# Latent attention with the plain rows of two heads and the rotary rows of four in shared tiles, and dense tiles at one address modulo 256

## What is computed

```python
h = x @ w_in[l]
c_q, c_kv, k_r, gate_a, q_d, k_d, v_d, gate_b, gates = _split_cols(h)
q_a = (_rms_norm(c_q, g_q[l]) @ w_q_up[l]).reshape(b, s, 8, 64 + 32)
q_a = jnp.concatenate([q_a[..., :64], _rotary(q_a[..., 64:], 32)], axis=-1)
kv = (_rms_norm(c_kv, g_kv[l]) @ w_kv_up[l]).reshape(b, s, 8, 64 + 64)
k_rope = _rotary(k_r, 32)                       # one for all heads
k_a = jnp.concatenate([kv[..., :64], jnp.broadcast_to(k_rope[:, :, None, :], (b, s, 8, 32))], axis=-1)
o_a = _dense_attention(q_a, k_a, kv[..., 64:], 1 / math.sqrt(96))   # softmax over all 512 keys
y_a = (o_a * jax.nn.silu(gate_a)) @ w_branch_a[l]
```

## Time and profile before

| | us |
|---|---|
| median of 3 runs (3389.13 to 3394.4) | 3393.46 |
| the profiled execution | 3391.75 |
| its span, first to last instruction | 3388.7 |
| TensorE busy | 3245.6 (96%) |
| VectorE busy | 2087.4 (62%) |
| GpSimd busy | 1347.1 (40%) |
| ScalarE busy | 1182.2 (35%) |
| mean granted TensorE clock, share of full | 0.977 |

### The profile page before, as it was taken

The page is one execution under the profiler, slowest core; times in us unless marked ns, Lnnn a source line. Parts: engine busy times, 40 slices in busy tenths (PEclk is TensorE's granted clock), DMA queues, the critical chain, the costliest instruction groups (busy, mean ns, idle before and its releaser), DMA issues.

```text
span 3388.7 us, 43762 instructions
## 1 busy us (share of the span) xinstructions
PE 3245.6 (96%) x16074; PEld 2541.7 (75%) x16074; DVE 2087.4 (62%) x2758; ACT 1182.2 (35%) x1808; POOL 1347.1 (40%) x565
## 2 busy tenths in 40 slices
PE   8999999999996999999998999999998999989998
PEld 6666787666785888778677888878887876878887
DVE  3877785777785444898378443464459964774422
ACT  3354423354423222433444222432233335332233
POOL 3302343302342445634143444634454531534454
PEclk9999999999997999999999999999998999999999
DMA  4524482524472332577232332333235771423332
GB/s 135 166 76 125 128 252 75 162 84 126 127 223 73 100 98 80 97 117 98 60 106 81 103 96 81 105 87 98 85 90 86 119 111 32 140 75 99 91 85 72
DMA packets 577891, 359.50 MB, mean 106 GB/s; under 512 B 48898, under 2 KB 528588, under 8 KB 577484
## 3 DMA queue, kind: packets, MB, share of 16 engines
q1 hardware_dynamic: 573908, 351.02, 40.3%
q10 hardware_dynamic: 3832, 6.42, 0.5%
HBM read 344.53 MB, written 10.49 MB: 105 GB/s over the span
## 4 chain that ended last, share of the span: by engine, by line
PE 51%; DVE 12%; SPq 2%; DMA 2%; issue 1%; ACT 1%; POOL 1%; ACTq 0%; POOLq 0%; DVEq 0%
PE bank L158 16%; PE bank L160 16%; PE bank L159 16%; SPq L1725 2%; DVE w_s L2349 2%; DMA w_raw<-in_mix_w_in_dram 1%; DVE xT L2464 1%; DVE z_s L2349 1%; DVE tt_s L2349 1%; DVE ct_s L2349 1%; PE bank L2030 1%; PE bank L2009 1%; POOL w_lo L152 1%; DVE y_s L2452 1%; DVE th_s L2471 0%
## 5 line engine op out<-in xcount | busy, mean ns | idle before, releaser
L152 POOL TENSOR_TENSOR w_lo<-w_raw,w_hi 128x1024 fp32r<-128x1024 f32 (+2 forms) x552 | 1339.1, 2432 | 2004.0 <-ACT w_hi L144 1996.0
L158 PE MATMUL bank<-xh,w_lo 128*128 128x512 f32 x2432 | 974.1, 401 | 46.4 <-DVE xl L2429 26.7
L160 PE MATMUL bank<-xh,w_hi 128*128 128x512 f32 x2432 | 962.3, 396 | 0.0
L159 PE MATMUL bank<-xl,w_hi 128*128 128x512 f32 x2432 | 960.8, 395 | 0.0
L144 ACT ACTIVATE w_hi<-w_raw 128x1024 fp32r<-128x1024 f32 (+2 forms) x552 | 565.9, 1028 | 788.9 <-PE bank L160 683.1
L158 PEld LDWEIGHTS bank<-xh,w_lo 128*128 128x128 f32 x2432 | 461.8, 190 | 167.4 <-issue 46.9
L159 PEld LDWEIGHTS bank<-xl,w_hi 128*128 128x128 f32 x2432 | 462.3, 190 | 104.5 <-issue 4.3
L160 PEld LDWEIGHTS bank<-xh,w_hi 128*128 128x128 f32 x2432 | 461.8, 190 | 99.3
L158 PE MATMUL bank<-HH_s,w_lo 128*128 128x512 f32 x704 | 276.1, 392 | 0.0
L160 PE MATMUL bank<-HH_s,w_hi 128*128 128x512 f32 x704 | 275.7, 392 | 0.0
L159 PE MATMUL bank<-HL_s,w_hi 128*128 128x512 f32 x704 | 275.0, 391 | 0.0
(11 more groups left out here) (509 smaller groups left out, 4392.1 us busy)
## 6 DMA issues: line engine op xcount, KB each, us to landing
w_raw<-in_ffn_w_in_dram SPq DMA_DIRECT2D x176, 512.0 KB, 3.9
m_raw_l<-in_mod_w_dram SPq DMA_DIRECT2D x128, 512.0 KB, 5.0
w_raw<-in_w_in_dram SPq DMA_DIRECT2D x80, 512.0 KB, 4.0
w_raw<-in_mix_w_in_dram SPq DMA_DIRECT2D x64, 512.0 KB, 9.9
w_raw<-in_ffn_w_out_dram SPq DMA_DIRECT2D x64, 384.0 KB, 3.4
w_raw<-in_ffn_w_out_dram SPq DMA_DIRECT2D x64, 320.0 KB, 3.2
m_half_l<-in_mod_w_dram SPq DMA_DIRECT2D x32, 256.0 KB, 2.7
w_raw<-in_w_out_dram SPq DMA_DIRECT2D x16, 512.0 KB, 4.8
```

What stands on the lines that cost most here:

```text
L152: nc.gpsimd.tensor_tensor(ring.lo[s][:, 0:width], ring.raw[s][:, 0:width], ring.hi[s][:, 0:width].bitcast(F32), ALU.subtract).then_inc(rin ...
L158: nc.tensor.matmul(out, wl, xh, start=start, stop=False)
L159: nc.tensor.matmul(out, wh, xl, start=False, stop=False)
L160: return nc.tensor.matmul(out, wh, xh, start=False, stop=stop)
```

## The change

It has three parts.

1. Tiles. `QT` becomes `QN` (4 tiles: plain rows of two heads, 128 rows) and `QR` (2 tiles: rotary rows of four heads), `KTr` becomes `KN` (4 tiles) and `KR` (one tile with the 32 rotary key rows four times). Block 3 now loads 32 columns, and `split_hi` and `split_lo` write them four times. The two query blocks are split in two instructions on each engine, which pack the columns. The query blocks take 3 groups of 6 matmuls of 128 columns each, the key block 4 of 3, and the swaps go from 16 to 10. The ScalarE spread and its semaphore go.
2. Scores. `scores_a(g)` now makes both heads of pair g: two matmuls of 64 rows at rows 0 and 64 of QN and KN, then two of 32 rows added onto them. It is issued after the transposes of an odd j, for g = j // 2 + 2. Score banks go from 3 to 4. The modulation's turn and column copy move (`half_turns`, `half_columns`).
3. Addresses. `eps` and `mod_cols` move behind xl, five small tiles become one of 32 bytes, and `mem.align()` puts the large tiles of both blocks at the ring's place modulo 256.

The diff, cut to its core:

```diff
-def split_hi(nc, act, ring, n, quad, s, width):
+def split_hi(nc, act, ring, n, quad, s, parts):
...
-    nc.scalar.activation(ring.hi[s][:, 0:width], ring.raw[s][:, 0:width], ACT.Copy).then_inc(ring.hi_done, 1)
+    for of, to in parts if isinstance(parts, list) else whole(parts):
+        ins = nc.scalar.activation(to(ring.hi[s]), of(ring.raw[s]), ACT.Copy)
+    ins.then_inc(ring.hi_done, 1)
...
+        if n == 3:
+            return [(lambda x: x[:, 0:KT * ROPE].rearrange("p (k a c) -> p k a c", k=KT, a=1).broadcast_to([P, KT, P // ROPE, ROPE]),
+                     lambda x: x[:, 0:BLK].rearrange("p (k a c) -> p k a c", k=KT, a=P // ROPE))]
+        if B_UP <= n < B_UP + 2:
...
+            return [(raw(slice(0, NOPE)), packed(0, NOPE)), (raw(slice(NOPE, QK)), packed(4 * NOPE, ROPE))]
...
-    half_turns = {17: 4, 30: 5}
-    half_columns = {20: 4}
+    half_turns = {16: 4, 30: 5}
+    half_columns = {17: 4, 31: 5}
...
     for j in range(NA):
-        hold(("s", j), j % 3)
-        hold(("t", j), 3 + j % 2)
+        if j in half_turns:
+            hold(("mod", half_turns[j]), 7)
+        hold(("s", j), j % 4)
+        hold(("t", j), 4 + 3 * (j % 2))
...
         for b in range(2):
             wh, wl = weights(B_UP + b, b)
             pe.wait_ge(s_cn, 2)
-            for h in range(4 * b, 4 * b + 4):
-                out = free(pe, ("qh", h))
+            for i, label in enumerate((("qn", 2 * b), ("qn", 2 * b + 1), ("qr", b))):
+                out = free(pe, label)
                 for k in range(2):
-                    c = slice(k * 384 + (h % 4) * QK, k * 384 + (h % 4) * QK + QK)
-                    last = mm3(nc, out[0:QK, :], wh[:, c], wl[:, c], cnh[:, k, :], cnl[:, k, :], k == 0, k == 1)
+                    c = slice(k * 384 + i * P, k * 384 + (i + 1) * P)
+                    last = mm3(nc, out, wh[:, c], wl[:, c], cnh[:, k, :], cnl[:, k, :], k == 0, k == 1)
...
+            out = [free(pe, ("s", 2 * g + side)) for side in range(2)]
+            c = slice(q * P, (q + 1) * P)
+            for side in range(2):
+                r = slice(side * NOPE, (side + 1) * NOPE)
+                nc.tensor.matmul(out[side], QN[r, p, c], KN[r, p, :], start=True, stop=False)
+            for side in range(2):
+                first = (2 * p + side) % 4 * ROPE
+                r = slice(first, first + ROPE)
+                nc.tensor.matmul(out[side], QR[r, p // 2, c], KR[r, :], start=False, stop=True).then_inc(s_sc, 1)
...
-            if j + 3 < NA:
-                scores_a(j + 3)
             pe.wait_ge(s_p, j + 1)
             turn_probs(("t", j), PX[j % 4])
+            if j % 2 and j // 2 + 2 < NA // 2:
+                scores_a(j // 2 + 2)
             if j >= 2:
                 attend_a(j // 2 - 1, (0, 1) if j % 2 == 0 else (2, 3))
...
         for j in range(NA):
             if j + 2 < NA:
                 negmax_a(j + 2)
+            if j in half_columns:
+                mod_columns(half_columns[j])
             wait_read(dve, ("s", j))
...
+    def align(self):
+        self.at += (self.phase - self.at) % self.LINE
```

More of the change, by code:

```diff
@@ L136, in fetch, with whole @@
     sp.dma_start(dst, src).then_inc(ring.load[s], 16)
-def split_hi(nc, act, ring, n, quad, s, width):
+def whole(width):
+    return [(lambda x: x[:, 0:width], lambda x: x[:, 0:width])]
+def split_hi(nc, act, ring, n, quad, s, parts):
     act.wait_ge(ring.load[s], 16 * quad + 16)
@@ L151, in split_lo @@
         pool.wait_ge(ring.used, n - (RING - 1))
-    nc.gpsimd.tensor_tensor(ring.lo[s][:, 0:width], ring.raw[s][:, 0:width],
-                            ring.hi[s][:, 0:width].bitcast(F32), ALU.subtract).then_inc(ring.lo_done, 1)
+    for of, to in parts if isinstance(parts, list) else whole(parts):
+        ins = nc.gpsimd.tensor_tensor(to(ring.lo[s]), of(ring.raw[s]), to(ring.hi[s]).bitcast(F32), ALU.subtract)
+    ins.then_inc(ring.lo_done, 1)
 def mm3(nc, out, wh, wl, xh, xl, start, stop):
@@ L495, in source @@
             if n < B_UP:
-                first = ([0, P, 2 * P, C_KR - NOPE] + [C_QD + m * P for m in range(4)] + [C_KD + m * P for m in range(4)])[n]
-                return w[:, :, first:first + P]
+                first = ([0, P, 2 * P, None] + [C_QD + m * P for m in range(4)] + [C_KD + m * P for m in range(4)])[n]
+                return w[:, :, first:first + P] if n != 3 else w[:, :, C_KR:C_KR + ROPE]
             if n < B_VD:
@@ L634, in mod_turn, with swap @@
             last.then_inc(s_mturn, 1)
-        def swap(i, src, rot, rows=slice(0, P)):
-            out = free(pe, ("r", i))
-            nc.tensor.matmul(out[rows, :], rot[rows, rows], src, start=True, stop=True).then_inc(s_rotated, 1)
+        def swap(i, src, rot):
+            nc.tensor.matmul(free(pe, ("r", i)), rot, src, start=True, stop=True).then_inc(s_rotated, 1)
         for s in range(4):
@@ L719, in turn_probs, with scores_a @@
             last.then_inc(s_tr, 1)
-        def scores_a(j):
-            p, q, side, h = place(j)
+        def scores_a(g):
+            p, q = divmod(g, TT)
             if q == 0:
[L725 to L730, removed]
+                pe.wait_ge(s_rot, 9 + p // 2)
+                wait_read(pe, ("qn", p))
+                wait_read(pe, ("kn", p))
+                if p == 0:
+                    pe.wait_ge(s_kr, 1)
+            out = [free(pe, ("s", 2 * g + side)) for side in range(2)]
[7 more added lines that the diff above has]
+                nc.tensor.matmul(out[side], QR[r, p // 2, c], KR[r, :], start=False, stop=True).then_inc(s_sc, 1)
         def attend_a(i, keys):
@@ L747, in attend_a @@
                         ins.then_inc(s_att, 1)
-        for j in range(3):
-            scores_a(j)
+        scores_a(0)
+        scores_a(1)
         for j in range(NA):
@@ L1014, in hi_next @@
                 act.wait_ge(ring.used, B_END + n - (RING - 1))
-                split_hi(nc, act, after.ring, n, 0, n, BLK)
+                split_hi(nc, act, after.ring, n, 0, n, width(n))
         for m in range(KT):
@@ L1435, in second_block @@
     pick = mem("pick", [P, HF], F32R)
+    mem.align()
     big = mem.at
@@ L2805 @@
 class Memory:
+    LINE = 256
     def __init__(self, nc, base, end):
-        self.nc, self.at, self.end, self.place, self.tag = nc, base, end, {}, ""
+        self.nc, self.at, self.end, self.place, self.tag, self.phase = nc, base, end, {}, "", 0
+    def align(self):
+        self.at += (self.phase - self.at) % self.LINE
     def __call__(self, name, shape, dtype, over=None, skip=0):
```

111 lines of the change are left out of this document (52 added, 59 removed).

## The result

The changed kernel takes 3401.55 us (median of 20 runs, 3397.41 to 3405.29), the kernel before 3394.86 (20 runs beside them, 3387.91 to 3400.93). The ratio is 1.0017, interval 1.001 to 1.0023: 3.4 to 7.8 us slower. The forecast was 0.6 us slower, so no change. The time lies in the range, but the change is real and the forecast had none. The profiled execution took 3403.22 us with a span of 3401.4, 12.7 more than before; 2.45 of these lie ahead of the first dense product (15.82 before, 18.27 after), among them a second wait of 1.43 us for a load of the input, which the kernel before does not have.

What follows compares the result with a forecast made beforehand. TensorE's own queue plus its few waits was taken to bound the kernel. To 3391.75 us came -24.4 (latent stage), -20 (addresses) and +45 (latent attention), +0.6 in all: about 3392 us, range 3369 to 3413.

Steps and rivals of the forecast that it cites:

- Part 1: Latent stage: fewer, wider products and fewer swaps take 16.43 us instead of 28.62, -12.2 us per layer, -24.4 for both.
- Rival (e): Latent stage: its saving is eaten by a wait for a split or a copy, up to 24 us, 3416; chance 0.04.
- Part 2: Latent attention, TensorE's own work: each score pair 1.06 us, a whole pair 4.48 against 4.16, +5 us per layer.
- Rival (d): Latent attention: the two 32-row products run one behind the other, 27 us, 3419 us, slower; chance 0.06.
- Part 3: Latent attention: TensorE waits for VectorE's normalise, 0.87 us in 14 groups (+12.2 per layer) and 0.67 eight times (+5.4).
- Rival (a): Latent attention: TensorE's new wait is smaller; half gone 3371 us, wholly hidden 3357; chance 0.28, of it 0.26 faster.
- rival (c): Latent attention: idle brings five stretches per layer of granted clock below full, 16 us, 3408 us, slower; chance 0.09.
- its own sign of being wrong: Latent attention: the prediction called itself wrong if the granted clock there falls under 0.95.
- part 4: Dense product and values stage: big tiles level modulo 256 bytes shorten the pitch, -20 us, between -15 and -26.
- Rival (b): Dense product: place in a partition is not the cause, the address term is 0, 3412 us, slower; chance 0.11.

Runs made afterwards that it cites:

- the normalise first: The changed kernel with VectorE's normalise of j (and a half chunk) moved ahead of the maximum for j + 2: 3362.88 us, ratio 0.9897 to the kernel before.
- the scores earlier: The changed kernel with a group's scores issued ahead of the transposes of the odd j instead of behind them: 3369.68 us, ratio 0.9924 to the kernel before.
- the waits filled: The changed kernel with matmuls of no use put into TensorE's waits in the latent attention: 3396.38 us, ratio 0.9997 to the kernel before.

## Why the prediction was wrong, step by step

**Part 1 held.** -12.2 per layer forecast, 28.62 to 16.55 measured, -12.1. Rival (e), a wait for a split or a copy, did not come.

**Part 2 held.** Both score pairs 1.06; the pair without waits 4.47 against 4.48. Rival (d) fell: the 32-row products run side by side, even four of them. This is what the Trainium skill, "TensorEngine Tiling (Array Packing)", section Key Properties, says of tiles, and rows now show it for 32 rows. The change of height costs about 0.20 where it was measured alone.

**Part 3 held as a mechanism and in size.** Waits at the places named, behind the releaser named, 0.85 and 0.68 from start to start for 0.87 and 0.67. Undone from VectorE's side they go (the normalise first), from TensorE's side they shrink by exactly the cover that is added (the scores earlier). Rival (a) fell.

**The step that failed: the clock was left out of the sum.** The prediction put parts 2 and 3 at 22.6 per layer and gave the clock to rival (c), at 0.09, with the argument that "the idle comes between full-speed 512-column scores". That argument holds for the steady loop and not for its start, where the profile of the changed kernel has 1.37 us idle, transposes alone, 0.54 idle. There the lower level begins and lasts 10 us. It costs 3.5 us in each layer (95.7 against 92.15 with the waits filled), 7.1 in both; the kernel before lost 1.6 in layer 0. So the attention windows are 95.7 where the prediction wanted 91 to 93, and their granted clock prints as 0.95, right at its own sign of being wrong. The rival priced its stretches by the one before, 1.6 each, and counted as decisive only from five in both layers together (8 us); two, each three times as long, cost 7.1 and were enough to turn no change into a clear one. What exactly brings the clock down is shown only so far: it fell in both layers of all four kernels that have 1.37 us idle, transposes alone and 0.54 idle at the start (the changed one, the one without the addresses and the two with x moved), and in none where the first wait was short (0.19), where scores stood behind it, or where the waits were filled.

**Mis-sized, if at all here: part 4.** The pitch came out as forecast, 228.75 to 226.67. The term was 20; the runs show 14 (9 to 19) and 15 (9 to 20) on the kernel before, and 17 (12 to 22) on the changed one. On the kernel before, the sum took for granted that the clock stays as it was. On the changed one no such loss shows: its mean clock of 0.9726 is 0.0025 under the kernel before, and its attention stages alone make that up (0.05 of 191 us less 0.02 of 71 us is 8 us of 3400, an estimate), so 20 is not excluded there. Rival (b) is out. It rested on the rule of the Trainium skill, "SBUF — State Buffer", section SBUF: two separate sides, that TensorE's port waits on nobody. The pitch follows the place of the two operands all the same, 226.67 to 233.7 ns for the same products, and the measurement decides.

With the measured sizes: -24.1 - 17.3 + 51.3 = +9.9. The two profiled executions fit that: 12.7 apart in span, 2.45 of it ahead of the first product, so 10.2. The medians show 3.4 to 7.8. Of the difference, 3.1 us is that the profiled execution before lies under its median (3391.75 against 3394.86) and 1.7 that the one after lies over its own (3403.22 against 3401.55); what differs between executions was not traced. With the forecast's own 20 for the addresses and the measured 51.3 the sum is +7.2, inside the interval: the clock in the attention is the term that turned the forecast wrong.

## What to carry to other kernels

When work on one engine is issued in pairs instead of one by one, look at the order of the engine that consumes it: a step that waits for the new pair must not stand ahead of the step that the producer needs next. Here one moved maximum was worth about 40 us. The first turns of a loop, before it runs evenly, want a sum of their own, with their waits written out: here the clock fell there and stayed low for 10 us behind waits of 1.37 and 0.54. A tile's place modulo 256 bytes against the tile that it is multiplied with was worth 1 to 3% of a dense product's pitch, and cost a few bytes of padding.

## What was not expected of the hardware

- The pitch of a 128x128 by 512-column matmul (of the fast kind used in the dense products) follows from where the moving operand lies against the stationary one modulo 256 bytes: level 226.67 ns, 64 behind 228.75 to 229.2, 64 ahead 233.3 to 233.7, 128 off 232.1 to 232.3. Only these four places were tried.
- Four 32-row float32 matmuls on four row groups cost what two do (2.13 against 2.11 with a full-height one behind). Each change of height costs about 0.20 us there, but none shows in front of the product with the values.
- A stretch at the lower clock is not always of one length: some 3 us within 221 to 225 in the kernel before, some 10 within 177 to 189 in the changed one. And the same wait of 0.88 us can be followed by one or not: in layer 1 the clock stayed at full before and fell with the addresses alone.
